# Two of six adaLN vectors in the opening, the others summed by VectorE in the even projections; neighbourhood attention with split value products

## What is computed

```python
def modulate(x, g, shift, scale):
    return rmsnorm(x, g) * (1.0 + scale) + shift
...
    for layer in range(DEPTH):
        mod_l = (jax.nn.silu(c) @ ada_w[layer] + ada_b[layer])[:, None, :]
        mod_c = (jax.nn.silu(c_ctx) @ ada_w[layer] + ada_b[layer])[None, None, :]
        sh1, sc1, g1, sh2, sc2, g2 = jnp.split(mod_l, 6, axis=-1)
        csh1, csc1, cg1, csh2, csc2, cg2 = jnp.split(mod_c, 6, axis=-1)
        h_l = modulate(x, norm1_g[layer], sh1, sc1)
        h_c = modulate(xc, norm1_g[layer], csh1, csc1)
...
        x = x + g1 * (o_l @ w_out[layer])
        x = x + g2 * sq_relu_mlp(modulate(x, norm2_g[layer], sh2, sc2), mlp_w1[layer], mlp_w2[layer])
```

```python
def mha_attend(q, k, v, bias=None, mask=None):
    s = jnp.einsum('bqhd,bkhd->bhqk', q, k).astype(jnp.float32) * (q.shape[-1] ** -0.5)
    if bias is not None:
        s = s + bias[None]
    if mask is not None:
        s = jnp.where(mask, s, -jnp.inf)
    p = jax.nn.softmax(s, axis=-1)
    return jnp.einsum('bhqk,bkhd->bqhd', p.astype(v.dtype), v)
```

## Time and profile before

| | |
|---|---|
| Median of 3 runs | 3914.34 us (3911.56 to 3914.55) |
| The profiled execution's own time | 3916.25 us |
| Its span in the trace | 3914.5 us |
| TensorE busy | 3586.2 us (92%) |
| VectorE busy | 2002.1 us (51%) |
| ScalarE busy | 1284.4 us (33%) |
| GpSimd busy | 174.4 us (4%) |
| DMA | 366.47 MB, mean 94 GB/s |

### The profile page before, as it was taken

One profiled execution on the slowest core, in us unless ns is written; L12 is line 12 of the kernel. 1 busy time (PEld: TensorE's weight loads), 2 busy tenths in 40 slices (PEclk: granted clock), 3 DMA queues, 4 the chain that ended last, 5 costly groups with the idle time before them and its releaser, 6 DMA issues. The chain is left out here.

```text
span 3914.5 us, 47315 instructions
## 1 busy us (share of the span) xinstructions
PE 3586.2 (92%) x17690; PEld 2863.7 (73%) x17690; DVE 2002.1 (51%) x2873; ACT 1284.4 (33%) x2279; POOL 174.4 (4%) x178
## 2 busy tenths in 40 slices
PE   8798798797899999999988979799799889999999
PEld 2586565786788888888877768577577668888887
DVE  2456564786663444443445455588544363333333
ACT  2453243564431111111125445466433341111111
POOL 0210010000120000000001000000000020000000
PEclk9899799898999999999999979799899899999999
DMA  8335564422321222221214344333344311111112
GB/s 313 132 129 188 143 136 89 113 76 87 88 83 57 69 62 70 60 60 55 66 51 155 140 142 143 97 73 73 81 101 92 108 54 46 46 48 48 54 54 65
DMA packets 431360, 366.47 MB, mean 94 GB/s; under 512 B 103381, under 2 KB 374117, under 8 KB 426085
## 3 DMA queue, kind: packets, MB, share of 16 engines
q1 hardware_dynamic: 431205, 364.42, 32.6%
HBM read 276.67 MB, written 87.69 MB: 93 GB/s over the span
## 5 line engine op out<-in xcount | busy, mean ns | idle before, releaser
L2033 DVE SCALAR_TENSOR_TENSOR xT<-ps,mods,xT 128x1024 f32<-128x1024 f32 x192 | 189.4, 1014 | 426.0 <-PE ps L2247 426.0
L2247 PE MATMUL ps<-e_gh,e_w2h 128*128 128x512 f32 x1280 | 356.7, 376 | 5.9 <-DVE e_w2l L2492 3.6
L2247 PE MATMUL ps<-e_gl,e_w2h 128*128 128x512 f32 x1280 | 352.8, 373 | 0.0
L2247 PE MATMUL ps<-e_gh,e_w2l 128*128 128x512 f32 x1280 | 352.2, 373 | 0.0
L2542 DVE TENSOR_TENSOR e_plain<-e_plain 128x1280 f32<-128x1280 f32 (+1 forms) x64 | 86.9, 1358 | 482.1 <-ACT e_plain L2407 482.1
L2247 PE MATMUL ps<-e_hl,e_w1h 128*128 128x512 f32 (+1 forms) x1200 | 327.2, 370 | 0.0
L2247 PE MATMUL ps<-e_hh,e_w1l 128*128 128x512 f32 (+1 forms) x1200 | 327.2, 370 | 0.0
L2247 PE MATMUL ps<-e_hh,e_w1h 128*128 128x512 f32 (+1 forms) x1200 | 327.1, 370 | 0.0
L2407 ACT ACTIVATE e_plain<-ps 128x1280 f32<-128x1280 f32 (+1 forms) x64 | 72.7, 1135 | 761.5 <-PE ps L2247 757.4
L2247 PEld LDWEIGHTS ps<-e_gh,e_w2h 128*128 128x128 f32 x1280 | 224.9, 190 | 55.5 <-DVE e_gl L2546 8.0
L2247 PEld LDWEIGHTS ps<-e_gh,e_w2l 128*128 128x128 f32 x1280 | 226.1, 190 | 43.6
(11 more groups left out here) (349 smaller groups left out, 7445.0 us busy)
## 6 DMA issues: line engine op xcount, KB each, us to landing
e_raw<-in_mlp_w SPq DMA_DIRECT2D x64, 512.0 KB, 4.1
e_raw<-in_mlp_w SPq DMA_DIRECT2D x128, 256.0 KB, 2.9
aw<-in_ada_w SPq DMA_DIRECT2D x12, 2048.0 KB, 9.0
rstd<-in_ada_w SPq DMA_DIRECT2D x64, 384.0 KB, 3.4
e_raw<-in_w_out SPq DMA_DIRECT2D x40, 512.0 KB, 3.9
qkC<-pc_stage SPq DMA_DIRECT2D x72, 192.0 KB, 2.7
hT<-pb_hb SPq DMA_DIRECT2D x10, 1024.0 KB, 5.4
pa_hb<-hT SPq DMA_DIRECT2D x10, 1024.0 KB, 5.0
```

What stands on the lines that cost most here:

```text
L2033: ins = k.nc.vector.scalar_tensor_tensor(out=x, in0=ps, scalar=k.mods[:, layer, gate, bass.ds(n, 1), w], in1=x, op0=ALU.mult, op1=ALU.add)
L2247: mm = pe.matmul(k.ps[:, SB * (e % 2) + b, 0:n], w[:, e % 2, f], m[:, f, c0:c0 + n], start=(f == 0 and x == 0), stop=(f == nf - 1 and x == 2))
```

## The change

The opening makes only vectors 0 and 1: four ada halves in place of twelve. Its order is now four x tiles, half 0, the six other x tiles, halves 1 to 3. Squares are taken and summed by chunks of tokens (512, 512, 256) and pairs of feature tiles, chunk 0 beside half 0, the others beside half 1. TensorE sums chunk 0 after half 1 and the others after half 2, with two matmuls a chunk where there was one; roots and reciprocals follow by chunk.

`project` takes `vectors`: "pb" makes vectors 2 and 3, "pa" 4 and 5, four groups of 512 columns in each, each of eight slices of 128 rows (256 KB), which are fetched into the weight buffers `raw` after the weights. VectorE multiplies and adds them (`vector_part`, two instructions a slice) at the end of the jobs that `slices_at` names, TensorE sums a group (`vector_sums`) after the products of the job behind the group's last slices and the turn that follows them, and VectorE adds the bias a job later (`vector_sum`). "pb" has one accumulator and uses PSUM bank 7, "pa" has two and bank 3, so its products have three banks.

`attend` takes `split` as an argument of its own: "ac" stays as it was, "ab" too, and "ad" keeps its scores and biases but splits its value products. In the diff below the functions that "ad" now also runs are those that "ac" ran before.

```diff
+VECTORS, OPENING_VECTORS = 6, 2
...
-        N_HALVES = 6 * D_MODEL // HALF
+        N_HALVES = OPENING_VECTORS * D_MODEL // HALF
...
-        steps = [("x", t) for t in range(XB)]
-        for n in range(N_HALVES):
-            steps += [("ada", n)] + [("x", t) for t in (XB + 2 * n, XB + 2 * n + 1) if t < NT]
-
-        X_DONE, SUM_AT = 3, 8
+        steps = [("x", t) for t in range(XB)] + [("ada", 0)] + [("x", t) for t in range(XB, NT)] + [("ada", n) for n in range(1, N_HALVES)]
+        PAIRS = KT // 2
+        squared_at, summed_at = {0: (0,), 1: (1, 2)}, {1: (0,), 2: (1, 2)}
...
+                def sums(c):
+                    if c == 0:
+                        pe.wait_ge(s.xcpA, NT)
+                        pe.wait_ge(s.xcpD, NT)
+                    pe.wait_ge(s.acc, (c + 1) * (PAIRS - 1))
+                    for a in range(2):
+                        mm = pe.matmul(k.ps[:, TB + c, 0:chunks[c][1]], k.ones[:], both(c)[:, a], start=(a == 0), stop=(a == 1))
                     mm.then_inc(s.sum, 1)
...
+                def squares(c, g):
+
+                    c0, n = chunks[c]
+                    if g == 0:
+                        act.wait_ge(s.xcpA, (c0 + n) // P)
+                        act.wait_ge(s.xcpD, (c0 + n) // P)
+                    here = c * (PAIRS - 1) + g - 1
+                    if g and here >= 2:
+                        act.wait_ge(s.acc, here - 1)
+                    nc.scalar.activation(both(c) if g == 0 else sq[:, here % 2, :, 0:n], k.xT[:, 2 * g:2 * g + 2, c0:c0 + n],
+                                         ACT.Square).then_inc(s.sq, 1)
+
+                def roots(c):
+                    c0, n = chunks[c]
+                    act.wait_ge(s.sum, c + 1)
+                    nc.scalar.activation(k.rstd[:, c0:c0 + n], k.ps[:, TB + c, 0:n], ACT.Sqrt, bias=k.eps[:],
+                                         scale=1.0 / D_MODEL).then_inc(s.root, 1)
...
+                def accumulate(c, g):
+                    n, here = chunks[c][1], c * (PAIRS - 1) + g - 1
+                    dve.wait_ge(s.sq, c * PAIRS + g + 1)
+                    if g > 1:
+                        dve.wait_ge(s.acc, here)
+                    nc.vector.tensor_tensor(both(c), both(c), sq[:, here % 2, :, 0:n], ALU.add).then_inc(s.acc, 1)
...
+def project(k, name, layer, w_in, col0, n_cols, units, keeps_h, sums_at=None, vectors=()):
...
-    RAW, LAG, MB, TB = 6, 2, 4, 4
+    RAW, LAG, TB, GC = 6, 2, 4, 512
+    MB, AB, ACCS = (3, 3, 2) if vectors and not keeps_h else (4, 7, 1)
+    NW, NG = len(slices), len(vectors) * D_MODEL // GC
+    PERIOD, FIRST = (N - U - 2) // NG if NG else 0, U
...
 
+    def slices_at(n):
+
+        g, y = (n - FIRST) // PERIOD, (n - FIRST) % PERIOD
+        if n < FIRST or g >= NG:
+            return range(0)
+        busy = PERIOD - 2 * (2 - ACCS)
+        return range(g * KT + min(KT, y * KT // busy), g * KT + min(KT, (y + 1) * KT // busy))
+
+    def group_after(n, later):
+
+        g = (n - later - FIRST) // PERIOD if n - later >= FIRST else -1
+        return [g] if 0 <= g < NG and any(a == g * KT + KT - 1 for a in slices_at(n - later)) else []
+
     def turned_after(n):
 
         return [n - LAG] if n - LAG in nth_head else []
...
+        if NG:
+            assert not any(group_after(N - 1 + y, 2) for y in range(1, 3))
+            free = nc.alloc_sbuf_tensor_at(f"{name}_aacc", [P, 2, GC], F32, offset=rope_at)
+            a_acc = [free[:], k.rstd[:, 0:2 * GC].rearrange("p (w n) -> p w n", w=2)][0:ACCS]
+            a_dram = k.ins["ada_w"][layer].rearrange("(k p) (g n) -> g k p n", p=P, n=GC)
+            a_group = [j * D_MODEL // GC + y for j in vectors for y in range(D_MODEL // GC)]
...
+                def fetch_vectors(a):
+                    x = NW + a
+                    if a < RAW:
+                        sp.wait_ge(s.wlo, x - RAW + 1)
+                    else:
+                        sp.wait_ge(s.aacc, 2 * (a - RAW + 1))
+                    sp.dma_start(raw[:, x % RAW], a_dram[a_group[a // KT], a % KT]).then_inc(wr[x % RAW], 16)
 
...
                         store_v(n)
+                    if n == FIRST - 1:
+                        for a in range(min(RAW, NG * KT)):
+                            fetch_vectors(a)
+                    for a in slices_at(n - 1) if NG else ():
+                        if a + RAW < NG * KT:
+                            fetch_vectors(a + RAW)
...
+                def vector_sums(g):
+                    pe.wait_ge(s.aacc, 2 * (g + 1) * KT)
+                    if g:
+                        pe.wait_ge(s.modd, g)
+                    for c in range(GC // P):
+                        for w in range(2):
+                            mm = pe.matmul(k.ps[:, AB, 2 * c + w:2 * c + w + 1], a_acc[g % ACCS][:, w, c * P:(c + 1) * P], k.ones[:, 0:1],
+                                           start=True, stop=True)
+                    mm.then_inc(s.asum, 1)
...
                 for n in range(N):
                     products(n)
                     for m in turned_after(n):
                         turn(m)
+                    for g in group_after(n, 1) if NG else ():
+                        vector_sums(g)
                 for m in rest:
                     turn(m)
...
+                def vector_part(a):
+                    x, g, f = NW + a, a // KT, a % KT
+                    dve.wait_ge(wr[x % RAW], 16 * (x // RAW + 1))
+                    if f:
+                        dve.wait_ge(s.aacc, 2 * a)
+                    elif g >= ACCS:
+                        dve.wait_ge(s.asum, g - ACCS + 1)
+                    for w in range(2):
+                        here = a_acc[g % ACCS][:, w]
+                        if f == 0:
+                            part = nc.vector.tensor_scalar(here, raw[:, x % RAW], k.sil2[:, f, w:w + 1], None, ALU.mult)
+                        else:
+                            part = nc.vector.scalar_tensor_tensor(out=here, in0=raw[:, x % RAW], scalar=k.sil2[:, f, w:w + 1],
+                                                                  in1=here, op0=ALU.mult, op1=ALU.add)
+                        part.then_inc(s.aacc, 1)
...
+                def vector_sum(g):
+                    HF = GC // P
+                    j, f0 = a_group[g] * GC // D_MODEL, a_group[g] * GC % D_MODEL // P
+                    dve.wait_ge(s.asum, g + 1)
+                    m, c = k.mods[:, layer, j, f0:f0 + HF], (layer * VECTORS + j) * KT + f0
+                    nc.vector.tensor_tensor(m, k.ps[:, AB, 0:2 * HF].rearrange("p (f a) -> p f a", a=2),
+                                            k.bcols[:, c:c + HF].unsqueeze(2).broadcast_to([P, HF, 2]), ALU.add).then_inc(s.modd, 1)
...
+                    for a in slices_at(n) if NG else ():
+                        vector_part(a)
+                    for g in group_after(n, 2) if NG else ():
+                        vector_sum(g)
...
+def attend(k, name, pieces, heads, load_head, parts, split, v_width, mix, mix_col, sink=None, bias=None, beside=None):
...
     NS, NB = len(head_steps), len(head_blocks)
     V, NU, BLOCKS = 2 * NS, 2 * NQ, 2 * NB
...
+            Unit(0, 512, v=512, v_dst=k.vA)], keeps_h=True, vectors=(2, 3))
...
+            Unit(512, 512, 8, ins["diff_k_g"][0], 1.0, True, k.qkA, 8)], keeps_h=False, vectors=(4, 5))
...
         layer_end(k, "e1", 1, SEQ, [(0, 512), (512, 512)], ins["w_out"][1], ins["mlp_w1"][1], ins["mlp_w2"][1])
```

More of the change, by code:

```diff
@@ L266, in turn_rows @@
                     mm.then_inc(s.colT, 1)
-                def sums():
-                    pe.wait_ge(s.acc, KT)
-                    for c, (c0, n) in enumerate(chunks):
-                        mm = pe.matmul(k.ps[:, TB + c, 0:n], k.ones[:], acc[:, c0:c0 + n], start=True, stop=True)
+                def sums(c):
[5 more added lines that the diff above has]
+                        mm = pe.matmul(k.ps[:, TB + c, 0:chunks[c][1]], k.ones[:], both(c)[:, a], start=(a == 0), stop=(a == 1))
                     mm.then_inc(s.sum, 1)
@@ L280, in _ @@
                             turn_rows(n - 1)
-                        if n == SUM_AT:
-                            sums()
+                        for c in summed_at.get(n, ()):
+                            sums(c)
                 turn_rows(N_HALVES - 1)
@@ L315, in _ @@
                     else:
-                        if X_DONE <= n < X_DONE + KT // 2:
-                            squares(2 * (n - X_DONE))
-                            squares(2 * (n - X_DONE) + 1)
+                        for c in squared_at.get(n, ()):
+                            for g in range(PAIRS):
+                                squares(c, g)
                         rows_out(n)
-                        if n == SUM_AT:
-                            roots()
+                        for c in summed_at.get(n, ()):
+                            roots(c)
             @block.vector
@@ L695, in inverse @@
                         nc.vector.reciprocal(k.rstd[:, q], k.rstd[:, q]).then_inc(s.rec, 1)
```

(19 more changed lines are left out.)

58 lines of the change are left out of this document (20 added, 38 removed).

## The result

| | us |
|---|---|
| before, median | 3914.45 (3911.56 to 3916.18, 4 runs) |
| after, median | 3948.74 (3947.96 to 3950.26, 4 runs) |
| ratio, with its 95% interval | 1.0091 (1.0077 to 1.0105) |
| after: profiled execution, its span | 3948.64, 3946.7 |

The account below looks back on a forecast made before the run. TensorE was taken to bound the opening, `pb` and `ad`. Opening -49, `pb` +56, `pa` +15 and `ad` -15 made +7 on the profiled 3916.25, so 3923.5, stated as 3921.5 for the median; range 3888 to 3944.

Parts of the forecast that it names:

- The opening: Opening: eight of twelve `ada` halves go, leaving 65.5 us against 114.6, 49 us less (46 to 52).
- The waits in `pb`: In `pb`, TensorE waits 30 us in all for the slices before the sums and 10 at the turned heads.
- The lock on scalar_tensor_tensor: In `pb`, slices and GpSimd's `hfull` shut each other out; without this `pb` would cost some 16 us less.
- rival (1): In `pb`, scalar_tensor_tensor escapes the lock and the clock hardly drops: `pb` costs 34, total 3897; chance 0.2.
- without the lock this one is 0.2: In `pb`, the turn wait at a group's first slices, 2.6 us, would be 0.2 without the lock.
- The clock: In `pb`, half-speed work after TensorE's long waits costs about 2.3 us a group, 9 in all.
- `pa`: Vectors in `pa`: stalls of 1.7, then 2.1 a group, with sums of 1.8 each: 15 us more (8 to 25).
- its bound of 70: Upper bound of the 56 us more forecast for `pb`, with a longer low clock.
- Rival (2): In `pb` and `pa`, each wait pulls the clock down for longer, as one-column sums follow it: 3945; chance 0.15.
- `ad`: Neighbourhood attention: split value products save 2.0 us a head, less a longer tail: 15 us less (10 to 18).

Follow-up runs that it names:

- clear_open: clear, with SyncE issuing the weights of `ada` 1 ahead of x tiles 8 and 9 in the opening; 3861.12 us, ratio 0.9865 to the kernel before.
- late_pool: Changed kernel; TensorE sums and VectorE adds the bias a job later, and in `pb` GpSimd's `hfull` waits for that job's slices; 3887.45 us.
- after_one: Changed kernel, with one eight-column matmul in place of each group's one-column matmuls, so the sums over partitions are left out; 3926.83 us.
- ad_only: Kernel before, with only the split value products in `ad`; 3896.05 us, ratio 0.9954 to the kernel before.
- clear: Changed kernel, with no slice in a tile's first job in `pb`, and in `pa` the sums a job later; 3864.50 us, ratio 0.9882 to the kernel before.
- warm: Changed kernel, with dense products that nobody reads ahead of each wait for `aacc`, 30 in `pb` and 8 in `pa`; 3947.97 us.

## Why the prediction was wrong

**The opening** was right in the changed kernel's trace: 66.7 us with a gap of 4.85 us ahead of the second `ada`, which then took 8.50, against 65.5 with 4 and 8.7. In part that was luck: the eight other traces of this opening have 68.7 to 70.3, beyond the 62 to 68 that I gave. I took the gap for granted; clear_open shows that it was the queue's order.

**The waits in `pb`** were right: 7.9 us against 8.1 behind the narrow jobs, 2.73 against 2.6 at the turns, 40.3 in all against 40. The lock on scalar_tensor_tensor, drawn from L680, was right too, and with it rival (1) fell. One clause was not: "without the lock this one is 0.2". Undisturbed, the turn behind the group's first slices still waits 0.6, and that behind its last ones 2.6 once the sums no longer wait first (late_pool).

**The clock** is the term that failed. I took 2.3 us in each group of `pb`, 9 in all, and nothing in `pa`; the trace has 26 and 14. With them `pb` came to 72.9 us more, over its bound of 70, and `pa` to 31.9, over its 25. For the dense products behind the long waits the 9 was right: they lose 9.5. Two parts were left at nothing. I took the low clock as a price of the long wait alone, by the earlier trace rows, which show it behind waits of 5 and 9 us, but it also fell behind three of the four turn waits of 2.7 us: 8.4 us. And I costed the work behind the wait as dense products at once, where the sums come first, which take 3.58 us instead of 1.95 at the low clock: 6.5 us.

Rival (2) said that each wait pulls the clock down for longer because the one-column sums follow it, and gave 3945. Its mechanism holds in `pa`: the stretches of low clock behind the four waits for `aacc` lose 11.8 us there, and 5.0 in after_one, where the sums are left out and two of the four stretches are gone. In `pb` it holds only for the sums' own time, since after_one keeps the rest; and the turn waits, which no sums follow, are not in it. That its time comes so near is luck as well, for without the 10 us of `pc` the measured time would be 3959. It stood at 0.15 because the earlier trace rows showed no short wait with a low clock. They showed no short wait at all, which is not the same, and the trace of before has one, in the weights' part of `pa`: after a long wait that ended at 306.5 the clock was back at 1.00, and then it is at 0.50 for 3.4 us behind waits of no more than 1.82 and 0.33 us.

```profile
311.00:314.30 3.30, 1.48 (x6) 0.59 (x4) 2.36 (x2) 2.78 (x5) 3.22 (x4) 1.00 1.06 418
314.40:317.80 3.40, 2.93 (x6) 1.67 (x6) 3.40 (x4) 0.83 (x2) 3.40 (x3) 0.50 0.97 369
```

**`pa`.** The waits were forecast at 8.0 us (1.7 and three of 2.1) and came to 11.9 more than before: the first was 4.76, since VectorE entered the first group already behind: it had cut weights until 350.6, and took up the group's first job at 361.4, 3.9 us after TensorE had ended it. The sums are 7.2 as forecast. The remaining 14 are the clock.

**`ad`** was right, 15.1 against 15, and ad_only shows it alone. In the trace of after a head lasts 28 to 29 us and VectorE works in 24 of them, near the forecast's 28.3 and 25.5. The misses add up: 17 of clock in `pb`, 14 of clock and 4 of waits in `pa`, 2 in the opening, less 10 of `pc`: 27, and 3921.5 plus 27 is 3948.5. The 10 of `pc` are not explained and stood in no sum.

**The verdict on the change.** Its plan was sound, and clear has it whole. The loss in `pb` came from eight jobs, two in each group: slices set into a tile's first job, where VectorE has `split_h` to do and GpSimd starts `hfull` as it ends, and sums asked for right behind the second of them. In `pa` it was the sums alone, asked for a job too early.

## What to carry to other kernels

Work that moves into another engine's idle time has to go where the idle time is within the period, not merely where the mean has room: here the same slices cost 72.9 or 16.3 us by the job that holds them. Cost each new wait of TensorE with the clock behind it: here 40 us of waits, with the thin sums behind them, brought 26 of clock, and the short ones were part of it. A queue that stands at a wait holds back every transfer behind it, so put first what nothing holds.

## What the runs showed of the hardware

- TensorE's granted clock fell to 0.50 (1.2 GHz) behind three of four waits of 2.7 us in after. In warm it fell behind 1.09 us of waiting with 1.95 us of one-column products after dense work, and in clear behind 0.66 us of waiting with 2.13 us of them; in both the group without a wait kept the full clock. Behind 7.9 us of waiting it stayed at 0.50 through the sums and some 5 us of dense products.
- Eight one-column fp32 matmuls (sixteen records) take 1.95 us at the full clock and 3.58 at the low one, and the clock was at 0.50 from before their start to after their end (after, 143 to 155).
- tensor_scalar with one SBUF input is locked against GpSimd as well: a pair took 3.02 us beside `hfull` and 0.88 without it.
